# A two-block model's kernel: full-width norm sums, a two-part gather of the experts' rows, a halved opening and four operations at other places

## The reference, cut to what matters

```
mod = silu(c) @ w_ada + b_ada            # six groups of 1024: shift, scale, gate, twice
u = rmsnorm(x) * norm1 * (1 + scale) + shift
hq, hf, hi, hg, aq, ak, av = split(u @ w_in)
mix = concat(hgrn2(...), diff_attention(...)) @ w_out
h = x + g1 * mix;   h = h + g2 * ffn(rmsnorm(h) * norm2 * (1 + sc2) + sh2)
x = rmsnorm(h) * final_norm_w            # first block ends

u = rmsnorm(x) * norm_mix
q, k, v, ... = split(u @ w_in_2)         # gated linear attention and retention
q_r, k_r = rotary(q, positions), rotary(k, positions)
x = x + merged @ w_out_2
t = rmsnorm(x) * norm_ffn
# each token takes 2 experts of 32 (one group of four): silu(t @ wg) * (t @ wu) @ wd, weighted and added
out = rmsnorm(x + y) * norm_final
```

## Time and profile before

| | us |
|---|---|
| median of 3 runs | 1357.98 |
| lowest, highest | 1357.75, 1358.46 |
| the profiled execution's own time | 1358.87 |
| its span, first to last instruction | 1356.9 |
| PE busy | 1296.5 (96%) |
| DVE busy | 580.3 (43%) |
| ACT busy | 471.4 (35%) |

### The profile page before, as it was taken

The page is one execution under the profiler, slowest core; times in us unless marked ns, Lnnn a source line. Parts: engine busy times, 40 slices in busy tenths (PEclk is TensorE's granted clock), DMA queues, the critical chain, the costliest instruction groups (busy, mean ns, idle before and its releaser), DMA issues.

```text
span 1356.9 us, 18862 instructions
## 1 busy us (share of the span) xinstructions
PE 1296.5 (96%) x8189; PEld 976.6 (72%) x8189; DVE 580.3 (43%) x935; ACT 471.4 (35%) x699; POOL 60.9 (4%) x58
## 2 busy tenths in 40 slices
PE   6899999999999999989999999899999999999996
PEld 3786889999999989978999999744344343444432
DVE  2666645444555488376654656522020111101112
ACT  3544444434444644444555544411011010101102
POOL 2021000000000122010020000000000000000000
PEclk8999979999998999999999999999999999999999
DMA  9767423675544344454245555799999999999993
GB/s 345 269 237 260 156 72 115 218 248 187 182 132 169 105 145 145 135 174 162 96 141 187 182 168 186 297 384 420 421 420 420 421 421 421 420 420 421 420 420 155
DMA packets 102340, 349.35 MB, mean 257 GB/s; under 512 B 5904, under 2 KB 9264, under 8 KB 77680
## 3 DMA queue, kind: packets, MB, share of 16 engines
q1 hardware_dynamic: 100912, 345.56, 67.4%
q0 software_dynamic: 1056, 2.47, 0.7%
q10 hardware_dynamic: 288, 0.10, 0.0%
HBM read 347.05 MB, written 1.05 MB: 257 GB/s over the span
## 4 chain that ended last, share of the span: by engine, by line
PE 88%; DVE 6%; ACT 3%; issue 1%; DMA 1%; POOL 0%; DVEq 0%; ACTq 0%; POOLq 0%
PE bank L550 42%; PE bank L894 16%; PE bank L929 8%; PE bank L751 4%; PE bank L764 4%; PE bank L577 2%; PE bank L465 2%; PE bank L507 2%; DVE WHL L1348 2%; ACT WHL L948 1%; PE bank L460 1%; PE bank L517 1%; PE bank L915 1%; PE bank L719 1%; PE bank L481 0%
## 5 line engine op out<-in xcount | busy, mean ns | idle before, releaser
L550 PE MATMUL bank<-XH,WHL 128*128 128x256 f32 x2928 | 542.2, 286 | 10.3 <-DVE WHL L1348 8.3
L550 PEld LDWEIGHTS bank<-XH,WHL 128*128 128x128 f32 x2928 | 463.3, 193 | 16.0 <-DVE WHL L1348 9.7
L550 PE MATMUL bank<-XL,WHL 128*128 128x256 f32 x1464 | 415.9, 284 | 0.0
L1348 DVE TENSOR_TENSOR WHL<-weights,WHL 128x1024 fp32r<-128x1024 f32 x223 | 281.7, 1278 | 219.5 <-ACT WHL L948 218.8
L948 ACT ACTIVATE WHL<-weights 128x1024 fp32r<-128x1024 f32 x223 | 232.1, 1054 | 223.2 <-PE bank L550 223.0
L550 PEld LDWEIGHTS bank<-XL,WHL 128*128 128x128 f32 x1464 | 283.2, 193 | 0.1
L550 PE MATMUL bank<-WHL,XH 128*128 128x512 f32 x320 | 105.3, 405 | 5.8 <-DVE WHL L1348 5.8
L2019 DVE TENSOR_TENSOR chainm<-bank,chainm 128x512 f32<-128x512 f32 x16 | 11.1, 692 | 171.7 <-PE bank L894 171.7
L894 PE MATMUL bank<-weights,arena 128*64 128x512 f32 x384 | 84.5, 592 | 0.0
L894 PE MATMUL bank<-arena 128*64 128x512 f32 x384 | 84.4, 592 | 0.0
L550 PEld LDWEIGHTS bank<-WHL,XH 128*128 128x128 f32 x320 | 62.2, 194 | 21.8 <-DVE WHL L1348 7.2
(11 more groups left out here) (314 smaller groups left out, 1144.6 us busy)
## 6 DMA issues: line engine op xcount, KB each, us to landing
weights<-in_w_in SPq DMA_DIRECT2D x58, 1024.0 KB, 5.1
weights<-in_w_ada SPq DMA_DIRECT2D x24, 1024.0 KB, 7.5
weights<-in_expert_w_gate SPq DMA_DIRECT2D x24, 1024.0 KB, 15.1
weights<-in_expert_w_up SPq DMA_DIRECT2D x24, 1024.0 KB, 16.3
arena<-in_expert_w_up SPq DMA_DIRECT2D x24, 1024.0 KB, 18.8
arena<-in_expert_w_down SPq DMA_DIRECT2D x24, 1024.0 KB, 21.2
weights<-in_expert_w_down SPq DMA_DIRECT2D x24, 1024.0 KB, 22.2
arena<-in_expert_w_gate SPq DMA_DIRECT2D x24, 1024.0 KB, 17.5
```

Of the source, the lines that this page charges most:

```text
L550: ins = e.matmul(o, l, r, start=first, skip_group_check=True, stop=g.part == g.parts - 1 and k == g.kc - 1 and n == 2)
L1348: e.tensor_tensor(lo, unit_weights(g, u), hi, ALU.subtract).then_inc(S.w_lo, 1)
```

## The change

- Opening: c has a tile of its own (`crow`), loaded first, then x. ACT squares the untransposed x with row sums, DVE inverts two columns and scales the identity with them (`diag`), and two products of ones by diag give rstd. hf and hq are loaded and multiplied in two halves of k; the first needs only modulation groups 0 and 2. The order is ada0, ada2, hf0, hq0, ada1, ada3, hf1, hq1. Ten of the small rows are loaded by POOL's queue; POOL's chain mask and two constants wait until x's rstd is made.
- The log and the scan of the forget gate stand behind the split of aq's first unit.
- The residual's norms use `norm_sums`: ones is the stationary operand, the squares (256 columns) the moving one; root and reciprocal work on 128 x 256, there is no spread. The root of the first block's final norm is taken later, in the retention's lane.
- `gated(L)` squares ahead of the yield.
- Positions and theta are loaded by POOL ahead of the second gated block's fills; the decay table stays where it was, with the gate weights' semaphore.
- The gather: `uhi` is the plain residual row rounded to fp32r (ACT), `ulo` the rest (DVE, `low_rows`), both times `pick` of type fp32r, 32 products a gather. The row's rms comes to the slots by four one-column products (`slot_norms`) and scales gate and hidden. In the first gather the high part runs ahead of the low part, in four banks.
- Of the experts' 16 slots 8 are now in the arena and 2 are late.

```diff
+            def norm_sums(i):
+                clear(4)
+                for k in range(KC):
+                    w.wait_ge(S.consts, 1)
+                    w.wait_ge(S.sq, KC * i + k + 1)
+                    ins = e.matmul(bank[4][:, 0:T], ones[:, :], scratch[:, k, :], start=k == 0, stop=k == KC - 1,
+                                   skip_group_check=True)
+                ins.then_inc(S.ss, 1)
...
-                        ins = token_sums(bank[4 + i], x[:, k, :], k == 0, k == KC - 1)
+                        ins = e.matmul(bank[4 + i][:, 0:T], ones[:, :], x[:, k, :], start=k == 0, stop=k == KC - 1,
+                                       skip_group_check=True)
...
             def choose(g):
                 w.wait_ge(S.m_slots, picked(g))
+                if g:
+                    slot_norms(g, 6)
+                banks = [4 + (q if g == 0 else q % 2) for q in range(4)]
+                def rows_of(u, q):
+                    for kk in range(2):
+                        k = 2 * q + kk
+                        for j in range(TT):
+                            ins = e.matmul(bank[banks[q]][:, kk * T:(kk + 1) * T], u[:, j, k * P:(k + 1) * P],
+                                           pick[:, j, :], start=u is uhi and kk == 0 and j == 0,
+                                           stop=u is ulo and kk == 1 and j == TT - 1, skip_group_check=True)
+                    return ins
+                if g == 0:
+                    w.wait_ge(S.rn, TT)
+                    for q in range(4):
+                        clear(banks[q])
+                        rows_of(uhi, q)
+                    w.wait_ge(S.rl, TT)
+                for q in range(4):
+                    if g:
+                        clear(banks[q])
+                        rows_of(uhi, q)
+                    rows_of(ulo, q).then_inc(S.m_ch, 1)
+                if g == 0:
+                    slot_norms(0, 3)
+            def slot_norms(g, b):
+                clear(b)
+                w.wait_ge(S.rn_v, 2)
+                for i in range(2):
+                    for j in range(TT):
+                        ins = e.matmul(bank[b][:, i:i + 1], pick[:, j, i * P:(i + 1) * P].bitcast(F32), ss[:, 4 + j:5 + j],
+                                       start=j == 0, stop=j == TT - 1)
...
+            e.transpose(bank[2][:, 0:KC], crow, ident[0:KC, 0:KC]).then_inc(S.rows_T, 1)
+            spin(3, 18)
...
+            spin(3, 10)
+            ada_sum(0)
...
+            ada_turn(0)
+            spin(3, 12)
+            ada_sum(1)
+            ada_turn(1)
+            spin(0, 14)
+            run(gemm("hf0"))
+            hq0 = gemm("hq0")
+            next(hq0)
+            ada_sum(2)
+            run(hq0)
+            ada_sum(3)
+            ada_turn(2)
+            ada_turn(3)
+            spin(4, 12)
+            run(gemm("hf1"))
+            run(gemm("hq1"))
...
             run(gemm("wo1"))
-            second_norm()
-            spin(7, 10)
+            norm_sums(0)
+            spin(5, 14)
...
             third_sums(range(4, KC))
-            spin(7, 10)
-            third_spread()
-            spin(7, 10)
+            spin(7, 16)
...
-                yield
                 for h in range(HEADS):
                     w.wait_ge(*L.at(L.out, HEADS))
                     e.activation(L.squares(h), L.oT[:, h * L.NV:(h + 1) * L.NV, :], ACT.Square).then_inc(L.sq, 1)
+                yield
...
+            hq1 = gemm("hq1", to_features(hq))
+            next(hq1)
+            split_to(by["aq"].unit0 + 1)
             w.wait_ge(S.gate_v, 6)
             e.activation(hf, hf, ACT.Ln).then_inc(S.gate_a, 1)
-            run(gemm("hq", to_features(hq)))
+            run(hq1)
...
             e.dma_start(gup, a["gla_gk_up_2"][0]).then_inc(S.d_gup, 16)
+            e.dma_start(posi, a["positions_2"].partition_broadcast(P).rearrange("p o t -> p (o t)")).then_inc(S.d_rotary, 16)
+            e.dma_start(theta, a["theta"]).then_inc(S.d_rotary, 16)
             run(gated(GL, []))
             w.wait_ge(S.oGn, 4)
-            e.dma_start(posi, a["positions_2"].partition_broadcast(P).rearrange("p o t -> p (o t)")).then_inc(S.d_rotary, 16)
-            e.dma_start(theta, a["theta"]).then_inc(S.d_rotary, 16)
-            e.dma_start(dec, a["decay"]).then_inc(S.d_rotary, 16)
+            e.dma_start(dec, a["decay"]).then_inc(S.d_gup, 16)
...
+            def low_rows(j):
+                w.wait_ge(S.rn, j + 1)
+                e.tensor_tensor(ulo[:, j, :].rearrange("p (k q) -> p k q", k=KC),
+                                xtok2[:, j, :].rearrange("p (q k) -> p k q", k=KC),
+                                uhi[:, j, :].bitcast(F32).rearrange("p (k q) -> p k q", k=KC), ALU.subtract).then_inc(S.rl, 1)
```

More of the change, by code:

```diff
@@ L242, in build @@
         AT = [b4.take([P, 384]) for _ in range(2)]
-        theta = b4.take([P, 1])
+        posi = c32[:, :, :].rearrange("p k q -> p (k q)").bitcast(I32)
+        theta = small[:, 88:89]
         assert b4.at <= ARENA - KC * T
@@ L253, in build @@
         assert b5.at <= 8192
-        utok = b5.take([P, TT, D])
+        full = Region(2048).take([P, TT, D])
         lg = b5.take([P, TT, 36])
         ss = b5.take([P, 8])
-        early5 = Region(b5.at)
-        wpT = [b5.take([P, T]) for _ in range(2)]
+        wpT = [hT[:, i, :] for i in range(2)]
         rt = b5.take([P, TT, 96])
@@ L414, in build @@
         S.r1, S.rs2 = sem("first_norm_sum"), sem("second_norm_sum")
-        S.u2, S.fin_a, S.fin = (sem("first_norm_" + n) for n in ("u", "rows", "out"))
+        S.u2, S.fin_a, S.fin_v, S.fin = (sem("first_norm_" + n) for n in ("u", "rms", "rstd", "out"))
         S.zz, S.z, S.dec_a, S.dec_v, S.gb = (sem("gla_" + n) for n in (
@@ L442, in build @@
         S.acc = sem("moe_added")
-        S.t_sq, S.t_sum, S.t_rms, S.t_rstd, S.t_out = (sem("last_norm_" + n) for n in ("squares", "sums", "rms", "rstd", "out"))
+        S.t_out = sem("last_norm_out")
+        NORMS = 2
         stored = sem("stored")
@@ L789, in tensor @@
-            spin(3, 8)
-            run(gemm("hf"))
-            run(gemm("hq"))
+            w.wait_ge(S.d_ident, 32)
+            e.transpose(bank[2][:, 0:KC], crow, ident[0:KC, 0:KC]).then_inc(S.rows_T, 1)
+            free[2] = (S.cT, 1)
+            spin(3, 18)
+            for j in range(TT):
+                w.wait_ge(S.d_x, 16)
+                for half in range(2):
+                    b = 4 + 2 * j + half
+                    for k in range(4):
+                        ins = e.transpose(bank[b][:, k * P:(k + 1) * P], xtok[:, j, (4 * half + k) * P:(4 * half + k + 1) * P],
+                                          ident[:, :])
+                    ins.then_inc(S.xT, 1)
+                    free[b] = (S.hT_v, 2 * j + half + 1)
@@ new lines, in tensor @@
+            spin(3, 10)
+            ada_sum(0)
+            w.wait_ge(S.consts, 1)
+            for j in range(TT):
+                w.wait_ge(S.x_v, 2 + j)
+                ins = e.matmul(bank[1][:, j * P:(j + 1) * P], ones[:, :], diag[:, j, :], start=True, stop=True)
+            ins.then_inc(S.x_p, 1)
+            free[1] = (S.x_a, X_RSTD)
+            w.wait_ge(S.d_rows, 3 * 16)
+            w.wait_ge(S.d_lam, 14 * 16)
+            e.transpose(bank[0][:, 0:NROWS], prow[0:NROWS, :], ident[0:NROWS, 0:NROWS]).then_inc(S.rows_T, 1)
@@ new lines, in first_split @@
+            def first_split(half):
+                for k in range(4 * half, 4 * half + 4):
+                    split_x(k, k, scratch[:, k, :], (S.nrm, k + 1), modc[:, k:k + 1])
+                    if k == 0:
+                        split_to(2)
+            first_split(0)
+            split_to(6)
+            ada_row(2)
+            ada_row(3)
+            first_split(1)
+            run(gemm("hf1", to_features(hf, func=ACT.Sigmoid)))
+            hq1 = gemm("hq1", to_features(hq))
+            next(hq1)
@@ L1776, in vector @@
[L1776 to L1788 removed]
+            modulation(1)
```

428 lines of the change are left out of this document (212 added, 216 removed).

## The result

| | before | changed |
|---|---|---|
| median, us | 1358.22 (4 runs) | 1334.63 (4 runs, 1333.15 to 1335.85) |
| profiled execution | 1358.87 | 1335.85, span 1334.1, clock 0.988 |

The ratio is 0.9834, 95% interval [0.9818, 0.985]: 23.6 us faster, where 28.8 were forecast; the range of 1321 to 1342 holds it. Such an interval is 2 to 3 us wide on either side, so two kernels whose whole times differ by 3 or 4 us are hardly told apart by them.

A forecast was written before the change was run, and what follows sets the result against it. PE was taken to bound the kernel up to the router, with loads close behind it in the experts. Terms -9.0, -3.8, -1.6, -6.3, -5.3 and -2.8 sum to -28.8, giving 1329.2 us at the median's level, range 1321 to 1342.

The forecast's parts named there:

- opening, with log and scan: Start to hq's end: first product at 28.0, and hole before aq gone; -9.0 us, bounds -6 and -12.
- squares ahead of the yield: Hgrn head sums: PE's 2.91 us wait for ACT's squares goes; -3.8 us, between -2.9 and -5.7.
- first norm: Residual's first norm: full-width sums, no spread, first scaled block at 227.2 instead of 228.75; -1.6 us, bounds +1 and -2.
- second norm: Residual's second norm: 32 wide records replace 64 one-column ones at half clock; -6.3 us, far bound +0.5.
- rotation: Rotation positions: DVE's 4.52 us DMA wait and PE's hole and slow clock go; -5.3 us, or -3.6.
- experts with the first gather: Router and experts: -1.3 from the first gather, -1.5 from later ones; -2.8 us, bounds +7 and -3.5.
- Rival (c): Norms: wide sums do not hold the clock, second norm gives nothing, first +1; 1339 us, chance 0.12.
- First gather: Router's end: slots 0.95 us later, but experts start at 886.9 instead of 888.3; -1.3 us.
- Later gathers: Gathers 2 to 8: 1.9 to 2 us less each, 13.3 for seven, only 1.5 showing before PE meets loads.
- Rival (a): Experts: the gather shows in full, 13.3 us instead of 1.5; 1317.4 us, chance 0.05.
- rival (b): Last expert pairs: PE waits for loads and its clock falls, up to 7 us; 1336 us, chance 0.12.
- rival (d): Experts: slow clock spreads there and makes the kernel slower than before; 1360 us or more, chance 0.03.

The follow-up runs named there:

- the kernel with yet less work: The changed kernel with the low part left out of gathers 2 to 8; 1335.53 us, ratio 0.9836.
- the last gather edit: Changed kernel with early first sine, 40 spins behind the second norm, and first gather's low part by token blocks, both subtractions behind the picks; 1331.07 us, ratio 0.9794.
- scan_first: The changed kernel with ACT's log and DVE's scan again ahead of the splits of aq's first unit; 1338.88 us, ratio 0.9857.
- positions_late: The changed kernel with positions and theta loaded behind the gated part again, the decay table still apart; 1334.92 us, ratio 0.9829.
- gather_high_twice: The changed kernel with the high part of gathers 2 to 8 multiplied twice; 1335.91 us, ratio 0.9842.
- fewer_spins: The changed kernel with 6 spin records instead of 24 ahead of the sums of modulation group 2; 1336.15 us, ratio 0.9838.
- four_edits: Changed kernel with early first sine, 40 spins behind the second norm, first gather's low part by token blocks, 6 opening spins instead of 24; 1332.06 us, ratio 0.9803.
- norm2_columns: The changed kernel with the second norm's sums alone made as before, by one-column records, with spread and spins; 1337.83 us, ratio 0.9863.

## Why the prediction held, and where its sum was off

| step | forecast | between the two traces | undone |
|---|---|---|---|
| opening, with log and scan | -9.0 | -6.1 (at product 384) | scan 2.5 |
| squares ahead of the yield | -3.8 | -5.8 (-6.7 in the gap itself) | 6.7 |
| first norm | -1.6 | -1.6 | |
| second norm | -6.3 | -5.7 | 5.7 |
| rotation | -5.3 | -2.9 | positions 0.0 |
| experts with the first gather | -2.8 | -1.1 (+0.7, -1.7) | |
| sum | -28.8 | -23.2, and 0.3 given back to product 2000 | |

The forecast held because the large terms were waits and slow sums that were really there. Part of its closeness is luck: the squares gave more than their term, the opening, the rotation and the first gather less. The scan, the squares, the second norm and the early positions were undone one at a time, and the later gathers tested from both sides. The halved opening as such, the first norm, the moved decay table and the change of the first gather were not, so their sizes are read from two traces only.

- **Opening.** Mis-sized mostly by the clock. hf's first product was put at 28.0, came at 29.99 in this execution and at 27.3 to 28.0 in six others, whose openings are the same. The step "24 spin records to 20.5" was priced at full clock, 2.6 us, and took 4.55. From there to the end of hq 31.8 were forecast and 32.2 measured. An early start is not wholly kept: with it the heads' stretch took 74.7 to 76.1 us instead of 74.4.
- **Squares.** The hole was rightly read; "the rest stays slow" was too careful. With no hole all sums ran fast, the root ended at 177.6 and the spread started at 177.87: the far bound of 5.7 is what came at the spread's start (5.8), and the spread itself took 2.87 instead of 3.76 us. Of these 6.7 us the stretch shows 5.8, as 0.9 was lost by the clock ahead of the heads.
- **First norm.** The 1.6 agree by some luck. Measured from the last product ahead of it, the first scaled block came 1.1 us earlier, where 1.5 were worked out, and the gap shrank by 1.4. In that gap 1.7 us were lost to the clock before and none in any kernel after, so how much the missing spread gives by itself is not shown. The 1.75 us reciprocal is there as foreseen.
- **Second norm.** Right but for 0.6 us: the first scaled block came 10.4 us behind the start of the sums, as worked out, the first product after another 1.7, 1.4 of them an idle PE, and then came 4 us at 0.66. Where the clock held there, the stretch took 76.9, 6.2 less than before and within 0.1 us of the forecast. Rival (c) is refuted: the wide sums ran at 1.00.
- **Rotation.** The wrong step is "its split ends near 584.3, before PE's last unit ends at 585.5". It left out that DVE comes to that split by way of ACT's sine, which stands in ACT's order behind evacuations that wait for PE. Of the two things that the prediction counted on here, the later wait for the decay table is, by elimination, what helped; the early positions did not. Early positions gave 0; of the 2.9 measured, 1.7 are less hole (3.61 before, 1.62 and 0.30 after), and the rest goes with the clock, which fell twice before and once after.
- **First gather.** The "128x1024 subtract of 1.28 us", taken from a contiguous one, took 2.01 with a stride of eight elements; the slots came 1.5 us later instead of 0.95, PE's wait rose to 3.08, and the high part ran at clock 0.63: +0.7 in place of -1.3. Where the clock held behind the same wait, the stage came to -0.8. So 1.4 of the miss are clock and some 0.6 the subtraction.
- **Later gathers.** Mechanism and size as forecast: 1.94 us a gather. Up to pair 9 PE runs 9.4 us ahead, in pairs 11, 13 and 15 the loads take 7.7 of them back, and 1.7 stay. The last load of up lands 433.4 us behind the first load into a released slot before and 433.1 after, the fixed distance that the prediction named. Rival (a) is refuted by the kernel with yet less work. Of rival (b) the first half came true, the clock's fall did not; nor did rival (d).
- **A wrong reading that did no harm.** "In the experts' part PE never waits" holds for loads alone: PE waited nine times for ACT to write the tile `masks`, 6.2 us in all, before and after alike.

The second root of the final norm in its later lane cost nothing: from product 3260 to 3300, across it, it takes 8.72 us before and after.

## What to carry to other kernels

When a second resource runs close behind the busy engine, its slack caps every saving in that engine's stream. Work out the slack first (here it let 1.5 of 13.6 us through), then prove it from both sides, with half the loads and with doubled work. When a late load is moved ahead, follow the waiting engine to its next partner too; here the next wait, an activation queued behind evacuations, kept half of the gain, and putting that one instruction ahead won 2.6 us. In these traces the clock was lost beside sums with one column (0.50 in the second norm), and wide ones ran at 1.00 and won 5.7 us even with a wide reciprocal. The gla heads' sums would be the next to widen (not tried). And before a stage's gain is put down to an edit, look for other kernels without the edit in which the clock held there: that took 1.4 of the 1.8 us from the last gather edit.

## What the runs showed that was not expected

- With the same instructions the clock falls in one execution and not in the next. Three places behind short holes or one-column sums (the opening's spins, the heads, the gla sums) cost 1.5 to 2.5 us each, or nothing; a hole of 2.83 us did in the kernel before and did not in scan_first. Which of them fall changes with microseconds won earlier. Kernels that reach product 384 at the same time repeat each other, though they differ elsewhere: positions_late and gather_high_twice (104.7) took 75.37 and 75.39 us to product 576, then 36.31 and 36.30; fewer_spins and four_edits (104.9) took 76.11 and 76.12, then 37.95 and 37.94. What decides stays open.
- Beside GpSimd's two-input operation two of DVE's small two-input ones took 2.7 and 2.8 us, 2.5 and 2.6 more than alone.
- The span ended 4.7 to 5.4 us behind the end of the last store's issue in all profiled executions but one, and 1.8 in that one (norm2_columns). No row shows why.
